# Gate rows of a modulation summed on VectorE ahead of one ones-matrix matmul, in a three-block transformer kernel

## The reference, cut to what matters

```
cond = silu(c)                                   # 1024 numbers
mod = cond @ w_ada[layer] + b_ada[layer]         # 1024 x 3072 matrix
shift, scale, gate = split(mod, 3)
h = rmsnorm(x, g_pre[layer]) * (1 + scale) + shift
y = mixer(h)                                     # layer 0: MLA and sliding window
x = x + gate * rmsnorm(y, g_post[layer])
```

## Time and profile before

| what | us |
|---|---|
| median of three executions | 1570.99 |
| lowest, highest | 1567.15, 1577.6 |
| profiled execution, its span | 1577.7 |
| PE busy in it | 1332.5 (84%) |
| DVE, ACT, POOL busy | 594.1, 425.1, 174.1 |
| share of PE in the chain that ended last | 72% |
| attention of layer 0, step 24 to its end | 289.6 to 414.9 |

### The profile page before, as it was taken

One profiled execution on the slowest core, in us unless ns is written; L12 is line 12 of the kernel. 1 busy time (PEld: TensorE's weight loads), 2 busy tenths in 40 slices (PEclk: granted clock), 3 DMA queues, 4 the chain that ended last, 5 costly groups with the idle time before them and its releaser, 6 DMA issues.

```text
span 1577.7 us, 14151 instructions
## 1 busy us (share of the span) xinstructions
PE 1332.5 (84%) x4792; PEld 778.1 (49%) x4792; DVE 594.1 (38%) x1395; ACT 425.1 (27%) x1078; POOL 174.1 (11%) x156
## 2 busy tenths in 40 slices
PE   1679989989897999899899898199989998688884
PEld 1455545645543443444565455054535464575552
DVE  4534323323253202344432311021246227476662
ACT  0133034533211003222451111042335337311001
POOL 0000003037200000000000000000000006534212
PEclk9989999966998999999999999599989999558876
DMA  9221311235404312211101213520011110000000
GB/s 322 72 80 47 114 54 54 85 133 183 107 1 106 54 32 55 75 53 56 51 4 63 73 42 62 146 95 29 13 41 40 54 54 1 27 1 1 14 14 27
DMA packets 60242, 99.93 MB, mean 63 GB/s; under 512 B 12062, under 2 KB 21995, under 8 KB 60172
## 3 DMA queue, kind: packets, MB, share of 16 engines
q1 hardware_dynamic: 54358, 93.56, 19.4%
q10 hardware_dynamic: 5814, 5.47, 1.2%
HBM read 94.93 MB, written 4.06 MB: 63 GB/s over the span
## 4 chain that ended last, share of the span: by engine, by line
PE 72%; DVE 12%; ACT 4%; another core or an unknown queue 3%; issue 3%; POOL 2%; ACTq 2%; DMA 1%; SPq 0%; DVEq 0%; POOLq 0%
PE PR L749 24%; PE SC L804 7%; PE PT L702 6%; PE OB L702 6%; PE OB L782 6%; PE SC L702 5%; PE PR L702 5%; PE PR L845 4%; PE PT L819 3%; PE SC L993 2%; DVE d L1506 2%; POOL arena L1406 2%; DVE d L1498 1%; PE PT L993 1%
## 5 line engine op out<-in xcount | busy, mean ns | idle before, releaser
L749 PE MATMUL PR<-ring,hT 128*128 128x512 f32 (+1 forms) x576 | 274.3, 588 | 37.1 <-DMA ring<-in_w_in 36.3
L782 PEld LDWEIGHTS OB<-arena,pts 128*128 128x128 f32 (+3 forms) x880 | 135.8, 206 | 111.4 <-issue 78.7
L1176 ACT ACTIVATE stage<-stage,nmax 128x256 f32<-128x256 f32 (+7 forms) x200 | 103.7, 519 | 297.6 <-DVE nmax L1754 279.5
L804 PE MATMUL SC<-arena 64*128 64x256 f32 (+15 forms) x432 | 152.4, 465 | 10.0 <-DVE nmax L1754 10.0
L749 PE MATMUL PR<-hT,ring 128*128 128x512 f32 (+1 forms) x304 | 155.6, 636 | 0.0
L749 PEld LDWEIGHTS PR<-ring,hT 128*128 128x128 f32 x576 | 99.5, 197 | 108.2 <-issue 63.0
L782 PE MATMUL OB<-arena,pts 128*128 128x64 f32 (+4 forms) x880 | 135.0, 284 | 16.9 <-ACT pts L1060 16.9
L1406 POOL TENSOR_TENSOR arena<-arena 128x192 f32<-128x192 f32 (+1 forms) x118 | 80.3, 681 | 547.9 <-PE OB L782 467.8
L819 PE MATMUL PT<-ident,stage 128*128 128x128 f32 (+3 forms) x440 | 89.8, 296 | 33.5 <-ACT stage L1155 15.9
L819 PEld LDWEIGHTS PT<-ident,stage 128*128 128x128 f32 (+3 forms) x440 | 58.1, 148 | 116.4 <-issue 51.8
L1060 ACT ACTIVATE pts<-PT 128x256 f32<-128x256 f32 (+7 forms) x200 | 80.7, 404 | 41.9 <-issue 22.3
(11 more groups left out here) (314 smaller groups left out, 1520.7 us busy)
## 6 DMA issues: line engine op xcount, KB each, us to landing
ring<-in_w_ada SPq DMA_DIRECT2D x12, 2048.0 KB, 9.9
ring<-in_od_w_in SPq DMA_DIRECT2D x8, 2048.0 KB, 13.8
ring<-in_w_in SPq DMA_DIRECT2D x5, 1536.0 KB, 6.9
ring<-in_ev_w_in SPq DMA_DIRECT2D x3, 2048.0 KB, 8.0
ring<-in_w_in SPq DMA_DIRECT2D x3, 2048.0 KB, 15.3
ring<-in_ev_w_out SPq DMA_DIRECT2D x2, 2048.0 KB, 7.8
ring<-in_od_w_out SPq DMA_DIRECT2D x2, 2048.0 KB, 8.0
ring<-in_w_out SPq DMA_DIRECT2D x2, 2048.0 KB, 8.5
```

What stands on the lines that cost most here:

```text
L749: mm = pe.matmul(dst, l, r, start=(k == 0), stop=(k == KT - 1))
L782: mm = pe.matmul(ob[:, h * w:h * w + w], pts[0:rows_, v % 2, n * P:n * P + P], vb, start=(n == 0), stop=(n == len(blocks) - 1))
L804: pe.matmul(SC[s % 2][:, 0:n], q, k, start=True, stop=True).then_inc(s_done, 1)
L1176: give(act.activation(pb[:, s % NP, 0:n], zm[:, s % 2, 0:n], ACT.Exp, bias=nmax[:, row, c:c + 1], scale=-1.0, accum_out=rsum[:, row, c:c + ...
```

## The change: what it does

DVE forms the sum over the eight blocks of an `adag` chunk, sum over k of W[k] * cond[k], in the 128 x 512 tile `d3`: one operation in each of eight consecutive attention steps (`gate_row`), first a tensor_scalar and then seven scalar_tensor_tensor, each reading a block of `ring` and `d3`. Then one matmul with a ones matrix (a broadcast column of `ones`) sums over the partitions and leaves the row in all 128 of them. The steps are 17 to 24 for chunk (0,4), 28 to 35 for (0,5), 38 to 45 for (1,4), and 48 to 55 for (1,5). `gate_row` stands in DVE's step behind the mask and `finish_group`, ahead of `finish_gates` and `tile_done`. An `adag` tile counts as one unit instead of eight, so 20 units are spread over steps 24 to 63, one in every second step. They end so: adag 0,0 in step 25, adac 1,0 in 33, adag 0,1 in 35, adac 1,1 in 43, adag 1,0 in 45, adac 1,2 in 53, adag 1,1 in 55, adac 1,3 in 63. The order of jobs and chunks is the same.

```diff
-UNITS = {"adac": 4}
+UNITS = {"adac": 4, "adag": 1}
+GATE_ROWS = {17: (0, 0), 28: (0, 1), 38: (1, 0), 48: (1, 1)}
...
+                if kind == "adag":
+                    pe.wait_ge(acg_s, list(GATE_ROWS.values()).index(name[1:]) + 1)
+                    pe.matmul(b[:, :], ones[:, 0:1].to_broadcast([P, P]), d3[:, :],
+                              start=True, stop=True).then_inc(pr_done, 1)
+                    yield
+                    return
                 for k in range(KT):
                     w = W[:, k, :]
-                    if kind == "adag":
-                        dst, l, r = b[:, :], cond[:, k:k + 1].to_broadcast([P, P]), w
-                    elif kind in FEATURE:
+                    if kind in FEATURE:
...
+            def gate_row(r_):
+
+                for n, (at, g) in enumerate(GATE_ROWS.items()):
+                    if not at <= r_ < at + KT:
+                        continue
+                    c, k = ("ada", g[0], 4 + g[1]), r_ - at
+                    W = w_view[c]
+                    if k == 0:
+                        dve.wait_ge(w_in[chunk_no[c] % RING], w_val[c])
+                        if n:
+                            used(dve, ("adag",) + list(GATE_ROWS.values())[n - 1])
+                        ins = ts(d3[:, :], W[:, 0, :], cond[:, 0:1], ALU.mult)
+                    else:
+                        ins = stt(d3[:, :], W[:, k, :], cond[:, k:k + 1], d3[:, :], ALU.mult, ALU.add)
+                    if k < KT - 1:
+                        link(ins)
+                    else:
+                        give(ins, acg_s, n + 1)
...
+                    if L == 0:
+                        gate_row(r_)
                     finish_gates()
```

More of the change, by code:

```diff
@@ L445, in two_block_kernel @@
         acp_s = sem("acp_s")
+        acg_s = sem("acg_s")
         acc_s = sem("acc_s")
@@ L725, in tile_matmuls @@
                 kind = name[0]
-                W = None if kind == "adac" else weights(chunk_of[name])
+                W = None if kind in ("adac", "adag") else weights(chunk_of[name])
                 b = begin(name)
```

## The result

The change makes the kernel slower: 1597.09 us (1595.22 to 1599.7, 4 runs) against 1574.3 for the kernel before (1567.15 to 1580.3), ratio 1.0127 with a 95% interval of 1.0082 to 1.0172. The forecast was 1585, range 1558 to 1603. The profiled execution has a span of 1593.2 us against 1577.7, 15.5 us more; it was the fastest of its four.

What follows compares the result with a forecast made beforehand. PE bounds the attention from step 24, at half clock in the window part. PE savings of -8 us and +22 us of POOL holds sum to +14 us, giving 1585 us, range 1558 to 1603.

Steps and rivals of the forecast that it cites:

- Part 1: Layer 0's attention from step 24, POOL left aside: matmuls PE is spared gain 5.1 and 2.8 us, together -8 us.
- the window part: Steps 32 to 63: 101.5 us before, 98.7 after at half clock, a gain of 2.8 us.
- The wait for weights: Moves from PE in step 44 to DVE in step 38: DVE stands 6 us, PE idles some 4.
- Part 2: 32 more DVE operations, 23 us in 32 steps, cost nothing by themselves because DVE has cover.
- Part 3: DVE rows reading two SBUF tensors wait for POOL's current operation in its chunk passes: +22.3 us.
- By pass: POOL's passes over chunks (1,1) from step 29, (1,2) about row 41, (1,3) about step 48: 7.4, 4.8, 10.1 us.
- the slack of 2.0 us: DVE delay PE does not feel in each POOL pass: DVE held 5.3 us, PE idle 3.32.
- The one with no hold: Operations on `ring` and `d3` not held, or DVE far enough ahead: -8 us stands, 1563 us; chance 0.13.
- The one with the clock up: Full clock in window steps, 19 us less: 1566 with holds (chance 0.07), 1544 without (0.11).
- The third: Clock falls earlier, after PE stands about 4 us near step 31; six steps double: 1592 us; 0.19 with the fourth.
- The fourth: DVE's queue in steps 38 and 48: weights wait costs 6 instead of 4, passes 2 more each: 1593; 0.19 with the third.
- The signs: About ten DVE operations above 1 us, PE idle behind ACT 25 us or more, PEclk 0.5, attention ending about 429.

Runs made afterwards that it cites:

- the control: Kernel before the change, with POOL writing zeros into the sums instead of its passes over the adac chunks: 1573.0 us, ratio 0.9956.
- The stretch without rows: Changed kernel with each adag as one ones-matmul reading block 0 and no gate rows on DVE: 1568.82 us, ratio 0.9936.
- late-rows kernel: Changed kernel, POOL's pass cut into 128 x 512 pieces, chunk (1,4)'s rows in steps 42 to 44, others one step earlier: 1570.72 us, ratio 0.9933; repeated 1570.73, 0.9959.

## Why the prediction was right, and by how much it was off

- **Part 1, without POOL.** I had 125.3 - 8 = 117.3 us; the stretch of the changed kernel without the pass is 116.1. Within it steps 24 to 31 took 20.0 us (289.05 to 309.04) where I had 18.7, and the window part 96.1 where I had 98.7. The waits for a row before the four ones-matmuls are 4.2 us (1.3 + 2.4 forecast), and such a matmul costs 1.84 with the clock down (317.84 to 319.68), where I had 1.71. The wait for weights did pass to DVE: it stood 7.4 us there and PE 5.6, where I had 6 and 4. Two slips in the working are small: the one-column units of the window part are thirteen and not fourteen (0.3 us), and PE stood still there a third time in the kernel before, 2.7 us behind ACT at 343.45, which the control has too. But this -8 is against a kernel that itself loses 7 us to POOL. Against the control, the change alone gives 2.2 us of stretch and 0.17% of the time, which is not clear of the noise.
- **Part 2.** Right where it can be compared. The stretch without rows (114.6 us) has POOL's passes and one hold in it, so it can't be set against the 116.1. Single steps can, where no hold and no wait for a row or for weights lies between: steps 27 to 31 take 11.20 us with a row in four of them (297.84 to 309.04, without POOL's pass) and 11.20 with none (296.91 to 308.11), steps 51 to 54 take 10.90 in both.
- **Part 3, the holds.** 27.8 us (143.9 - 116.1) where I had 22.3. By pass, from the distance between the two kernels' step starts: 8.8 (7.4 forecast), 6.9 (4.8), 11.7 (10.1); the 0.4 left lie in the wait for weights. This is the mis-sized term, and its weak part is the slack of 2.0 us for each pass. Put into the same sums, the three measured costs leave a slack of 0.6, -0.1 and 0.4. The 2.0 came from one hold alone, as DVE's 5.3 us less PE's idle 3.32; the control shows that this hold cost 7.0 us of stretch. In the first pass PE's values of 8 blocks behind the hold ran at half clock, 1.97 us instead of 1.00. In the third three operations were held in one step, the tensor_scalar among them (2.45 us instead of 0.49), and there was no slack left: 12.0 us of holds on DVE (6.30 + 3.41 + 1.96, and 0.35 of the next row), 11.7 on PE.
- **The 128 x 4096 product holds.** No row before showed it; 6.21 and 6.86 us do now. The tensor_scalar, which I left out of the sum, is held as well, 2.45 us beside an addition. The Trainium skill, SBUF — State Buffer, "Who interferes with whom", lets a tensor_scalar contend when it is in a two-port mode; the 2.45 us agree, but no run shows which mode it was in.
- **Rivals.** The one with no hold gave 1563, 8 us under the kernel before; without POOL's pass the changed kernel is 10 us under it by the medians (1568.75 against 1578.92), but the holds are there. The one with the clock up is out by the 0.50. The third is right in part: with the holds the clock fell at 311.6, at the end of PE's 4.4 us of idle time in step 31; without POOL's pass it was 1.00 to 312.6, in step 34. It did not double six steps. The fourth, no slack for PE, comes nearest: it adds 2 us to the wait for weights, which measured 6.0 in the changed kernel, and 2 to each pass, 28.3 in all against 27.8. It had a share of 0.19 with the third.
- **The signs.** Those named beforehand came: ten operations of DVE (rows, `fr`, `tok` and the tensor_scalar) took over 1 us, PE's waits behind ACT's copies grew from 7.2 to 31.4, PEclk was 0.50, and the wait for weights passed to DVE. The attention ended at 432.3 and not 429.
- **The sum.** +14 forecast, +15.5 by the two spans, +18.6 by the stretch, and +20 by the ratio. The chance that it would be slower by more than 1% was put at 0.44; the ratio is 1.27% up, its interval from 0.82%. The range was wide enough to take in no change at all, so that the time fell in it says little; the rows and the runs without POOL's pass carry the mechanism. There is luck in the -8, too: it counts the loss of the kernel before's own hold (3.3 us of PE idle) and 4.7 us of the change's own gain, where 7.0 and 2.2 were measured, two misses that cancel.

## What to carry to other kernels

Before work is moved from one engine to another, look in the trace for an operation that is much longer than its equals, and ask what another engine did at that moment: one row of 2.36 instead of 0.17 us foretold here a loss of some 28 us. When DVE and POOL both work from SBUF, give DVE one SBUF input (the other in PSUM, as `d<-OB,fr` has it; no run moved an input there) or cut POOL's operations: here the late-rows kernel has a stretch of 116.2 us with pieces of 512 columns (1.04 us and up), and of 121.9 with pieces of 1024 (1.9 us and up). And do not count removed matmuls at full price where the steps left are narrow: look what clock such steps have had.

## What the hardware showed that was not expected

- A hold costs twice: the 3.32 us of PE idle in the earlier trace rows were worth 7.0 us of stretch. The granted clock fell during it and stayed at 0.50 for 20.5 us, against 10.3 in the control; steps 51 and 52 took 2.94 us each instead of 1.61 and 2.03.
- Thirty-two matmuls of 508 columns without use lengthened the stretch by 1 us (3.6 by the ratios, not clear of the noise), while the mean clock in 312 to 400 rose from 0.50 to 0.83.
- POOL's product over 128 x 512 takes 1.04 us, over 128 x 4096 it takes 7.02: cut eightfold it costs 8.3 us. The first pass, which lies ahead of the stretch, takes 18.7 us cut and 15.7 uncut: 1.3 of the 3 us are the product's, the rest is the additions' and the gaps'.
